# A fused three-block fp32 transformer: layer norms and the units behind them by halves of 128 tokens

## The reference, cut to what matters

```python
h = x * (1.0 + sc_m) + sh_m
y = mixer(h, ...)
x = layer_norm(ALPHA * x + (1.0 + g_m) * y, ln_mix_g[i], ln_mix_b[i])
h = x * (1.0 + sc_f) + sh_f
y = (silu(h @ w_gate[i]) * (h @ w_up[i])) @ w_down[i]
x = layer_norm(ALPHA * x + (1.0 + g_f) * y, ln_ffn_g[i], ln_ffn_b[i])
```

## Time and profile before

| | |
|---|---|
| median of 3 runs | 1215.04 us (1214.33 to 1215.46) |
| the profiled execution: time | 1214.23 us |
| the profiled execution: span | 1212.4 us |
| mean granted TensorE clock | 0.984 |
| TensorE / VectorE / ScalarE busy | 96% / 73% / 51% |

### The profile page before, as it was taken

How to read it: one execution, slowest core, us unless ns; L and a number is a source line. 1 busy time by engine, 2 the same in 40 slices (tenths; PEclk the granted TensorE clock), 3 DMA queues, 4 the chain that set the end, 5 groups by cost and what they waited for, 6 DMA issues and landing times.

```text
span 1212.4 us, 22780 instructions
## 1 busy us (share of the span) xinstructions
PE 1159.5 (96%) x8644; PEld 1097.0 (90%) x8644; DVE 879.2 (73%) x1486; ACT 615.2 (51%) x989; POOL 70.3 (6%) x134
## 2 busy tenths in 40 slices
PE   4999889999999999899999999999999999999997
PEld 4898669999888898899998799999999999999997
DVE  5799878998888975696554677686765776877743
ACT  4447656444436666644443456434443646555532
POOL 0101110211111300000000000000000000000000
PEclk9899989999999999999999999998899999999999
DMA  9957765999774744475555434433332453645531
GB/s 362 364 206 246 243 208 203 365 392 361 291 295 141 247 152 139 157 276 199 196 179 185 153 132 140 157 109 119 121 127 87 170 189 119 214 173 181 200 139 35
DMA packets 43131, 241.67 MB, mean 199 GB/s; under 512 B 5152, under 2 KB 7584, under 8 KB 20400
## 3 DMA queue, kind: packets, MB, share of 16 engines
q1 hardware_dynamic: 28912, 191.29, 44.1%
q0 software_dynamic: 14144, 49.37, 11.5%
HBM read 237.48 MB, written 1.06 MB: 197 GB/s over the span
## 4 chain that ended last, share of the span: by engine, by line
PE 82%; DVE 8%; ACT 5%; issue 3%; DMA 1%; SPq 0%; POOL 0%; DVEq 0%; ACTq 0%; POOLq 0%
PE acc L1919 19%; PE acc L1920 19%; PE acc L1921 19%; PE aux L2029 3%; PE aux L2031 3%; PE aux L2030 3%; PE aux L2409 2%; ACT whi L589 1%; DVE wlo L1047 1%; DMA x<-xT 1%; PE aux L1921 1%; PE aux L1919 1%; PE aux L1920 1%; ACT free_hlo L634 1%; PE aux L2073 1%
## 5 line engine op out<-in xcount | busy, mean ns | idle before, releaser
L1919 PE MATMUL acc<-hhi,whi 128*128 128x256 f32 (+3 forms) x1976 | 569.1, 288 | 8.4 <-DVE hlo L1068 5.8
L1920 PE MATMUL acc<-hlo,whi 128*128 128x256 f32 (+3 forms) x1976 | 561.9, 284 | 0.0
L1921 PE MATMUL acc<-hhi,wlo 128*128 128x256 f32 (+3 forms) x1976 | 559.1, 283 | 0.0
L1047 DVE TENSOR_TENSOR wlo<-raw,whi 128x1024 fp32r<-128x1024 f32 x338 | 412.6, 1222 | 187.5 <-ACT whi L589 185.8
L589 ACT ACTIVATE whi<-raw 128x1024 fp32r<-128x1024 f32 x338 | 356.5, 1056 | 183.7 <-PE acc L1921 113.5
L1919 PEld LDWEIGHTS acc<-hhi,whi 128*128 128x128 f32 x1976 | 375.8, 190 | 14.0 <-DVE hlo L1068 8.2
L1921 PEld LDWEIGHTS acc<-hhi,wlo 128*128 128x128 f32 x1976 | 377.4, 191 | 0.0
L1920 PEld LDWEIGHTS acc<-hlo,whi 128*128 128x128 f32 x1976 | 376.2, 190 | 0.2
L1076 DVE CUSTOM_DVE_ANT_0 lev<-lev,vec 128x1024 f32<-128x1024 f32 x56 | 71.6, 1279 | 2.2 <-DMA lev<-side_weights 2.2
L2031 PE MATMUL aux<-wlo,ahi 128*128 128x512 f32 x176 | 69.5, 395 | 0.0
L2029 PE MATMUL aux<-whi,ahi 128*128 128x512 f32 x176 | 69.4, 394 | 0.0
(11 more groups left out here) (368 smaller groups left out, 1510.7 us busy)
## 6 DMA issues: line engine op xcount, KB each, us to landing
raw<-weights SPq DMA_DIRECT2D x176, 1024.0 KB, 4.9
lev<-side_weights POOLq DMA_DIRECT2D x76, 512.0 KB, 6.6
x<-ln_rows POOLq DMA_DIRECT2D x6, 512.0 KB, 5.8
big<-side_weights POOLq DMA_DIRECT2D x4, 512.0 KB, 5.7
big<-qkv POOLq DMA_DIRECT2D x32, 64.0 KB, 2.8
x<-gate_rows POOLq DMA_DIRECT2D x3, 512.0 KB, 7.0
x<-xT SPq DMA_DIRECT2D x1, 1024.0 KB, 11.4
raw<-weights SPq DMA_DIRECT2D x2, 512.0 KB, 4.9
```

The costliest lines, as they stand in the source:

```text
L1047: v.tensor_tensor(wlo[:, m % SPLIT, :], raw_unit(i, m), whi[:, m % SPLIT, :].bitcast(F32), ALU.subtract).then_inc(lo_ready, 1)
L1919: mm(o, whi[:, u % SPLIT, w], hi, start=start, stop=False, skip_group_check=True)
L1920: mm(o, whi[:, u % SPLIT, w], lo, start=False, stop=False, skip_group_check=True)
L1921: return mm(o, wlo[:, u % SPLIT, w], hi, start=False, stop=stop_, skip_group_check=True)
```

## The change

Norms 0, 1 and 2 and the three units behind each run by token halves. After half 0 is scaled, TensorE turns its eight feature tiles (`turn_half`: even tiles into one bank, odd ones into the next), ScalarE and VectorE make its h in pairs of tiles, and TensorE does the three units' products for half 0, with 128 columns. Half 1 is turned after the third pair of half 0 and follows in the same way. On ScalarE the first two makes stand ahead of the statistics of half 1. VectorE prepares the affine after the second bank, and scales half 1 in one piece behind four makes. `out1` has depth 2. The splits that were held behind down0 (two) and the one behind out1 go ahead in the usual order, into `shelf` places in `ahi` and `alo` that are idle by then. The scratch of the gates and the output of the squares move to other buffers. Dummy matmuls are 12, 2 and 5. In ffn0 the third unit starts two pairs late, in odd no longer late. Norm 3 only has its semaphore counts renumbered. Left out of the diff: the old bodies of `make_hi` and `make`, the same `place_free` and `high_weights` put into the callers, renumbered waits, and calls that went.

```diff
@@ -251,7 +251,12 @@
         def token_tiles(tok):
             return tokens[:, D * tok:D * tok + D].rearrange("p (q k) -> p k q", k=KT)
 
-        x_flat, tokens, scratch = flat(x[:, :, :]), flat(xa[:, :, :]), flat(tile[:, :, :])
+        x_flat, tokens = flat(x[:, :, :]), flat(xa[:, :, :])
+
+        def scratch(L):
+            return flat(qkv[:, 0:4, :] if L % 2 else qkv[:, 20:24, :])
+
+        squares_out = big[:, 2, 1088:1088 + D]
         ROW_GATE, ROW_GAIN, ROW_SHIFT = x_flat[:, 0:D], x_flat[:, D:2 * D], x_flat[:, 0:D]
...
@@ -465,14 +470,43 @@
 
         SEG = {name: n for name, n, _ in SEGMENTS}
         ROW_SEGMENTS = ["out0", "down0", "out1", "down1"]
-        ROW_DEPTH = [1, 3, 1, 3]
+        ROW_DEPTH = [1, 3, 2, 3]
 
         def held(seg, j, on_scalar):
 
-            if seg not in ROW_SEGMENTS:
-                return False
-            deep_ = ROW_DEPTH[ROW_SEGMENTS.index(seg)] > 1
-            return j >= SEG[seg] - (2 if deep_ else 0 if on_scalar else 1)
+            if seg == "out0":
+                return j == SEG[seg] - 1 and not on_scalar
+            return seg == "down1" and j >= SEG[seg] - 2
+
+        def shelf(m):
+
+            after = {n: START[n][1] + SEG[n] for n in ("down0", "out1")}
+            if m == after["down0"] + 1:
+                return flat(ahi[:, 11:15, :]), flat(ahi[:, 15:19, :]), START["down0"][1] + 19
+            if m == after["down0"] + 2:
+                return flat(alo[:, 10:14, :]), flat(alo[:, 14:18, :]), START["down0"][1] + 19
+            if m == after["out1"] + 2:
+                return flat(alo[:, 2:6, :]), flat(alo[:, 6:10, :]), START["out1"][1] + 5
+            return None
+
+        def high_weights(i, m):
+            place = shelf(m) if i is None else None
+            return place[0][:, 0:UNIT] if place else whi[:, m % SPLIT, :]
+
+        def low_weights(i, m):
+            place = shelf(m) if i is None else None
+            return place[1][:, 0:UNIT] if place else wlo[:, m % SPLIT, :]
+
+        def place_free(eng, i, m):
+
+            place = shelf(m) if i is None else None
+            if place:
+                eng.wait_ge(units_done, place[2])
+            elif m >= SPLIT:
+                eng.wait_ge(units_done, lin(i, m - SPLIT + 1))
+
+        HALVES = 3
+        TURNS = [4 * n for n in range(HALVES + 1)]
 
         def partial_sum(tok):
...
-                H = L + 1
+            def make_hi(L, g):
+
+                tok, pair = divmod(g, 4)
                 act.wait_ge(affine_ready, L + 1)
...
+                act.wait_ge(tr_mm, TURNS[L] + 2 * tok + 2)
+                if tok:
+                    act.wait_ge(h_ready, 8 * (L + 1) + g - 3)
+                n = 2 * pair + 1
+                st(A(tile[:, pair, P:2 * P], aux[2 * tok + 1][:, P * pair:P * pair + P], ACT.Identity,
+                     scale=affine[:, L, 0, n:n + 1], bias=affine[:, L, 1, n:n + 1]))
+                st.wait()
+                act.wait_ge(h_f32, 8 * L + g + 1)
+                A(hhi[:, 2 * pair:2 * pair + 2, P * tok:P * tok + P],
+                  tile[:, pair, 0:T1].rearrange("p (k t) -> p k t", k=2), ACT.Copy).then_inc(hhi_ready, 1)
 
             def token_norm(L):
...
@@ -642,12 +672,16 @@
                 st(A(shift_of(0), minus_mean(0), ACT.Copy, scale=rstd[:, 0:1]))
                 st.wait()
                 A(tokens[:, 0:D], tokens[:, 0:D], ACT.Identity, scale=rstd[:, 0:1], bias=shift_of(0)).then_inc(u_first, 1)
-                if ROW_DEPTH[L] > 1:
+                if L == 3:
                     split(None, last + LEAD - 1)
+                else:
+                    make_hi(L, 0)
+                    make_hi(L, 1)
                 spread(1)
                 A(rstd[:, 1:2], log_var(1), ACT.Exp, scale=-0.5).then_inc(rs_ready, 1)
-                if ROW_DEPTH[L] > 1 and L < 3:
-                    split(None, last + LEAD)
+                if L < 3:
+                    for g in range(2, 8):
+                        make_hi(L, g)
 
             def norm(L, t, eps, bank):
...
@@ -1156,46 +1185,58 @@
                     if b % 2:
                         st.wait()
                         gather(b // 2)
-                if L < 3:
-                    sections_made(MODULATION[L + 1][0] * 6 + MODULATION[L + 1][1] + 2)
-                    prepare_affine(L)
-                held_split(last + LEAD - (1 if ROW_DEPTH[L] > 1 else 0))
-                dve.wait_ge(rs_ready, L + 1)
-                scale(0, KT // 2)
-                scale(KT // 2, KT)
+                    if b == 1 and L < 3:
+                        sections_made(MODULATION[L + 1][0] * 6 + MODULATION[L + 1][1] + 2)
+                        prepare_affine(L)
                 if L == 3:
+                    held_split(last + LEAD - 1)
+                    dve.wait_ge(rs_ready, L + 1)
+                    scale(0, KT // 2)
+                    scale(KT // 2, KT)
                     for n in range(KT):
-                        dve.wait_ge(tr_mm, 8 * L + n + 1)
+                        dve.wait_ge(tr_mm, TURNS[3] + n + 1)
                         v.tensor_scalar(x[:, n, META:T2], aux[n % 4][:, 0:T1], V("ln_g", 8 * L + n), V("ln_b", 8 * L + n),
                                         ALU.mult, ALU.add).then_inc(x_norm, 1)
                     held_split(last + LEAD)
                     return
+                H = L + 1
                 dve.wait_ge(affine_ready, L + 1)
-                H = L + 1
...
+
+                def make(g):
+                    tok, pair = divmod(g, 4)
+                    n = 2 * pair
+                    dve.wait_ge(tr_mm, TURNS[L] + 2 * tok + 1)
+                    if tok:
+                        dve.wait_ge(h_ready, 8 * H + g - 3)
+                    v.tensor_scalar(tile[:, pair, 0:P], aux[2 * tok][:, P * pair:P * pair + P], affine[:, L, 0, n:n + 1],
+                                    affine[:, L, 1, n:n + 1], ALU.mult, ALU.add).then_inc(h_f32, 1)
+
+                def make_low(g):
+                    tok, pair = divmod(g, 4)
+                    k, t = slice(2 * pair, 2 * pair + 2), slice(P * tok, P * tok + P)
+                    dve.wait_ge(hhi_ready, 8 * H + g + 1)
+                    low(hlo[:, k, t], tile[:, pair, 0:T1].rearrange("p (k t) -> p k t", k=2), hhi[:, k, t])\
+                        .then_inc(h_ready, 1)
                 make(0)
+                make(1)
+                make_low(0)
                 make(2)
-                make_low(0)
-                if ROW_DEPTH[L] > 1:
+                make_low(1)
+                make(3)
+                if L == 0:
                     held_split(last + LEAD)
-                make_low(1)
-                make(4)
+                dve.wait_ge(rs_ready, L + 1)
+                scale(0, KT)
                 make_low(2)
                 make_low(3)
+                make(4)
+                make(5)
+                make_low(4)
                 make(6)
-                for n in range(4, KT):
-                    make_low(n)
+                make_low(5)
+                make(7)
+                make_low(6)
+                make_low(7)
 
             def restore(L, piece):
...
@@ -1944,24 +1985,41 @@
                         ins = products(j, k, m0 + j)
                         if k == KT - 1:
                             ins.then_inc(units_done, 1)
-                    if turned is not None:
-                        for k in range(4):
-                            turn_tokens(turned, k, hhi_ready, 8 * turned + 8)
                     for k in range(KT):
                         pe.wait_ge(ready, before + k + 1)
-                        for j in range(first - 1 if k < late else first):
+                        for j in range(first):
                             step(j, k)
-                        if turned is not None and k + 4 < KT:
-                            turn_tokens(turned, k + 4, hhi_ready, 8 * turned + 8)
-                        if late and k == late - 1:
-                            for done in range(late):
-                                step(first - 1, done)
+
+                def first_halves():
+                    def step(j, tok, pair):
+                        t = slice(P * tok, P * tok + P)
+                        if tok == 0 and pair == 0:
+                            pe.wait_ge(lo_ready, m0 + j + 1)
+                            if turned % 2 == 0 and j >= 2:
+                                pe.wait_ge(nm_ready, 2 * turned + 2)
+                            if a0 + j >= 4:
+                                acc_read(pe, None, a0 + j - 4)
+                        for k in (2 * pair, 2 * pair + 1):
+                            ins = three(acc[(a0 + j) % 4][:, t], m0 + j, k, hhi[:, k, t], hlo[:, k, t], k == 0, k == KT - 1)
+                        if tok == 1 and pair == 3:
+                            ins.then_inc(units_done, 1)
+                    turn_half(turned, 0)
+                    for tok in range(2):
+                        for pair in range(4):
```

(58 more changed lines are left out.)

45 lines of the change are left out of this document (15 added, 30 removed).

## The result

The kernel with the change takes 1264.57 us, median of four runs (1260.11 to 1275.91), beside 1214.72 us (1214.33 to 1215.46) for the kernel before: a ratio of 1.0424, interval 1.0354 to 1.0494. It is slower, as forecast, but by 50 us where 14 were forecast, and outside the range. The profiled execution took 1266.45 us, 52.2 over the 1214.23 of before.

What follows compares the result with a forecast made beforehand. TensorE, busy 96% of the span, was taken as the bound; 3.8 + 6.0 + 1.6 + 2.9 = 14.3 us on the profiled 1214.23 gave 1228.5, 1229.3 on the median, called 1229; range 1217 to 1240.

Steps and rivals of the forecast that it cites:

- The sign: Whole kernel: the change makes it slower, given 0.87, against 0.08 for faster and 0.05 for the same.
- the price of a half product: First three units behind each norm: the weight load sets the pace, 0.113 us per 128-column product; chance 79%.
- half price: Rival for the first units' products: a narrow product costs half a wide one, 0.059 us; about 1205 us, 7%.
- 0.086: Rival for the first units' products: an in-between step in us, part of the load hidden; 1217 to 1218 us, 8%.
- two passes: Rival for the first units' products: fp32r under 256 columns runs as fp32 does, 49 us on top; about 1278 us, 6%.
- Why going ahead does not pay: Three units behind each norm: 144 narrow products for 72 wide, first to last 17.2 us where about 9.4 before.
- The start of the first product: Norms 0 to 2: the first product comes 2.67 us after ScalarE's scaling of half 0 ends.
- VectorE's queue of three splits ahead of norm 1's gates: Norm 1: VectorE does three splits in a row, 1.15 us each, so the first gate starts at 362.2, not 359.93.
- The whole of norms 0 and 1: Fourth unit later by 3.8 us in norm 0 and 6.0 in norm 1, clock loss apart; norm 2 was given 2.9.
- I let the clock stay up, in norm 0 too: Norms 2 and 0: no clock loss assumed, with norm 2's idle times of 0.6 and 1.5 us.
- the +1.6 of norm 1: Norm 1: clock lost after idle times of 1.6 and 1.5 us, 3.4 us at the half level, costing 1.6 us.
- a second norm could lose the clock: Variation allowed inside the main case, in which the weight load decides (79%); its variations spanned 1224 to 1236 us.

Runs made afterwards that it cites:

- e2: The changed kernel with three dummy matmuls added between turning half 0 and the first product, and more ahead of turning in norms 0 and 1: 1225.12 us, ratio 1.0085.
- E5: e2, but both halves are turned before the first product, with dummies between, and products are 256 columns wide again: 1218.81 us, ratio 1.0031.
- E1: The changed kernel, but each half product streams its 128 columns twice, with the same number of products: 1230.2 us, ratio 1.013.

## Why the prediction was right and wrong

*The sign, and the price of a half product: right.* At full clock the step in norm 0 of after is 0.112 us (82 steps from 186.00 to 195.15), single instructions, against the 0.113 taken from 64 columns; in e2 it takes 17.05 us from first product to fourth unit. Neither half price, nor 0.086, nor two passes is seen. Of the Trainium skill's 81 ns at 128 columns ("TensorE: Matmul & The Clock Gate", "Back-to-back issue gap"), no stretch here shows it; the measurement decides for 0.112, for these products.

*Why going ahead does not pay: right.* The products of half 0 start earlier, but those of half 1 cost as much again as whole products would have: 432 of 0.112 for 216 of 0.118 is 22.9 us more, before eight transposes move in among them. E5 takes 6.3 us of it back.

*The start of the first product: right.* Turning to product is 173.51 - 170.82 = 2.69 us. The forecast had 2.67 from the end of the scaling, so 2.60 from the turning (its terms add up to 2.65 and not 2.67). *VectorE's queue of three splits ahead of norm 1's gates: right*, in VectorE's timeline of after, which answers to the earlier trace rows:

```profile
366.74 1.23 DVE L1078 TENSOR_TENSOR wlo<-raw,whi 128x1024 fp32r<-128x1024 f32 x1 [1.49 <-ACT whi L621]
367.88 1.22 DVE L1078 TENSOR_TENSOR ahi<-raw,ahi 128x1024 fp32r<-128x1024 f32 x1
369.01 1.22 DVE L1078 TENSOR_TENSOR alo<-raw,alo 128x1024 fp32r<-128x1024 f32 x1
370.15 0.68 DVE L1155 TENSOR_TENSOR qkv<-aux,x 128x512 f32<-128x512 f32 x1
```

The gate comes 3.41 us behind the first of the splits (3 x 1.15 forecast). The whole of norms 0 and 1 comes out within 0.2 us in e2, norm 2 is 1.0 better than forecast: its first gate already comes 0.9 us earlier (496.61, for 488.0 and the 9.5 of the norms ahead).

*The step that failed: "I let the clock stay up, in norm 0 too", and with it the +1.6 of norm 1.* I saw both idle times and took from the earlier trace rows that a fall lasts 3.4 us at half. That row has whole products behind the fall. With half products behind it the clock stayed at half for 34.1 us in norms 1 and 2, and 10.2 in norm 0; and norm 2 fell with idle times of 0.5 and 1.5 us, which I held to be harmless. The mechanism, a loss of the clock behind the idle times, stood in the text for norm 1 only; its length was out by a factor of ten, and its place by two norms. No rival had it; that a second norm could lose the clock was allowed for, but at a price that ended at 1236. E1 and e2 are the proof: change only the columns, or only the idle time, and 34 and 39 us of the 50 go.

*The total.* Counted from the first gate of norm 0 (165.07, 164.41 and 164.92 in before, after and e2), the fourth unit of norm 2 comes 11.6 us later than before in e2, for the 12.7 forecast without the clock, and 46.5 later in after. The falls cost the 34.9 between, and 1.6 more until the clock is back at 561 (19 products in 3.8 us): 36.5 us where the forecast had 1.6. Behind that, after takes 4.8 us longer, at a lower clock:

```profile
561.00:1264.65 703.65, 686.68 (x5340) 665.21 (x5339) 462.60 (x680) 333.92 (x464) 6.19 (x10) 0.98 0.45 155
513.60:1212.42 698.82, 681.89 (x5339) 660.49 (x5337) 464.87 (x683) 334.77 (x466) 6.18 (x10) 0.99 0.45 157
```

The first line is after, the second before. With the head start of 0.7 the sum is 11.6 + 36.5 + 4.8 - 0.7 = 52.2, as measured. That the 4.8 belong to the change is not shown: the falls of the third block differ from run to run.

## What to carry to other kernels

Where weight loads set the pace, a product of half the columns costs nearly the time of a whole one (0.112 for 0.118 us here), so a split of the moving side pays only if it uncovers more idle time than it adds loads. Price a fall of the clock by the work that follows it, not by the length of a fall that some other work followed; and before narrow products above all, fill the last microseconds with dummy matmuls, those between the transposes and the first product too. When a change loses, try its harmless parts by themselves: out1's early split and depth, with the idle times filled, beat the kernel before by 0.6%. And where runs of one kernel scatter, set each time beside its granted clock before explaining a difference.

## What was unexpected of the hardware

A TensorE without a gap did not get the full clock back: 30.65 us of products of 128 columns and eight transposes at 1.2 GHz, then full clock 3.5 us after products of 256 columns had begun. At full clock the same narrow products did keep it (e2, some 17 us in each norm). In norm 0 of after it came back at 185.6, among half products, just behind the eight transposes of half 1; in norms 1 and 2 the same transposes brought nothing. Why is open. The 16 us between single runs of that kernel follow the granted clock too: 1260.11 us had a mean of 0.960, 1275.91 us one of 0.946. The narrow product's 0.214 us at half clock also says that whatever sets its pace, the weight load by the rows, slows with TensorE's clock.
